# Six pairs of gate projections by seven products, ahead of the linear attention, with the gates parked in DRAM

## The chip, the cores and the metric

The kernel runs on one core of one Trainium2 chip. The metric is the device time of one execution in microseconds, as a median over runs. Engines are named as the profile names them: PE (matmuls), PEld (its weight loads), DVE, ACT, POOL (elementwise work) and SP, whose queue issues the DMAs.

## What is computed

One decoder layer over 1024 tokens of 1024 channels, in float32: a SwiGLU block, a token mixer, a second SwiGLU block, each behind a norm with shift and scale. The change lies in the mixer:

```python
proj = u @ w_in
gq, gk, gv, gr, ga, dq, dk, dv, gates = jnp.split(proj, split_points(IN_SIZES), axis=-1)
ya = gla(gq, gk, gv, ga, gla_alpha_w2, gla_alpha_b)
ya = rmsnorm(ya, gla_head_norm) * jax.nn.silu(gr)...
ya = ya.reshape(B, S, GLA_VW) @ w_branch_a
yb = diff_attention(dq, dk, dv, lq1, lk1, lq2, lk2, lam_init)
yb = rmsnorm(yb, diff_head_norm) * (1.0 - lam_init)
yb = yb.reshape(B, S, DIFF_VW) @ w_branch_b
g_a, g_b = jnp.split(jax.nn.sigmoid(gates), N_BRANCH, axis=-1)
return (g_a * ya + g_b * yb) @ w_out
```

`gates` has 2048 columns: 8 groups of 128 for branch 0 (the linear attention, `ya`) and 8 for branch 1 (the differential attention, `yb`).

## The kernel before

Everything is kept channel-major: a tile has 128 channels as partitions and tokens as columns, in two halves `hf` of 512 tokens. Each float32 operand of a large matmul is split in two numbers, `hi` (rounded) and `lo` (the rest), and a product takes three matmuls (hi by hi, hi by lo, lo by hi). A **unit** is 128 output columns of weights against all tokens: 8 groups `k` of channels, 3 products, 2 halves, 48 matmuls of 128x512 (`project`, L2457; matmuls at L2468). Its weights are loaded by SP into one of three slots of `w_raw` (L766), and POOL makes `w_hi` (L997) and `w_lo` (L1003, two instructions) of a slot once the unit that held it is done (`split_unit`). SP issues the load of unit u once unit u-3 is split.

The two SwiGLU blocks multiply with the seven-product scheme instead (Strassen's, in Winograd's form): a pair of column groups is one tile of seven products of 12 matmuls each (L2507), 84 where two units would take 96. It needs sums of the token blocks once (T1 to T4, made by DVE, ACT and POOL) and, for each tile, four sums of weights, seven roundings (ACT, L1297), seven `lo` (POOL, L1030) and some additions of the results. The first weights of a tile can be loaded only when POOL has read those of the tile before.

The mixer, in order. `norm(1)`: DVE makes the normalized pieces, ACT rounds them to `u_hi`, and DVE (even k, L1809) and POOL (odd k, L1051) make `u_lo`. PE begins on them at once in `first_units` (L2419): the narrow projection `ga` and the two units of `gq`, half 0 and then half 1, k by k, each k behind its `u_lo`. Then 16 small matmuls of the decay (`z`, L2604), the units of `gk` and `gv`, the linear attention, the differential attention with further units as filling, and the branches.

The branches: `branch_product(br, m)` is 24 matmuls of a branch's output against the columns m of its weights; one split of weights serves two m. It alternates with gate units: for each pair of m first the two gate units (L2468), then the two branch products. Gates (0,0) to (0,2) are made earlier. ACT takes the sigmoid of a gate out of PSUM (L1649), DVE multiplies it with the branch product (L2338 for branch 0, L2341 for branch 1) and for branch 1 adds both branches in `z[m]` (L2343). Between the branches ACT rounds the four blocks of `yb` (`high_y`, L1411) once the last product of branch 0 is done, because they take the place of `ya`'s, and DVE makes their `lo` (`low_y`, L2059). Late in branch 1, before m=6, DVE makes `lo` of z[0] to z[5] (`low_z`, L2059), and of z[6], z[7] at the end; the output projection `w_out` follows k by k behind it.

Each engine works through its instructions in the written order. SP writes the residual `h` (4 MB) to DRAM near the start of the mixer (L917) and reads it back among the branches (L931).

Of the kernel before, what the change touches and what calls it, by code (L numbers as in the profile page):

```python
# [13 lines left out]
P = 128  # L14
# [36 lines left out]
U_OUT = U_BRANCH + 24  # L51
# [3 lines left out]
for _br in range(2):  # L55
    for _i in range(0 if _br else 2, 4):
        _order += [("gate", _br, 2 * _i), ("gate", _br, 2 * _i + 1), ("w", _br, _i)]
BRANCH_UNIT = {what: U_BRANCH + n for n, what in enumerate(_order)}
MB = 0
MIX_LOADS = MIX_UNITS // SLOTS  # L60
# [17 lines left out]
def build_program(nc, a, out):  # L78
    ctx = ExitStack()
    with ctx:  # L80
# [86 lines left out]
        with stage() as st_:  # L167
            at(st_, "pad_out", [P, FRONT // 4])
            o_tile = [at(st_, f"o_tile{j}", [P, D])[:] for j in range(8)]
        u2_b, u3_b, g0_b, g1_b = [bufs[:, j, :] for j in range(4)]  # L170
# [18 lines left out]
        un_b = [far[:, j * HALF:(j + 1) * HALF] for j in (14, 15, 16, 17)]  # L189

        def un_place(n, hf, k):

            if n == 1:
                return un_b[piece(n, hf, k) % 4]
            return unf[:, hf + 2 * (k // 4), k % 4, :]
# [24 lines left out]
        low = far[0:2 * GLA_RANK + 1, 5 * S:6 * S]  # L220
# [40 lines left out]
        sig_b = [far[:, 4 * S + j * HALF:4 * S + (j + 1) * HALF] for j in range(2)]  # L261
        h_dram = nc.dram_tensor("h_dram", (P, KT * S), F32).ap()
# [20 lines left out]
        h_dve = sem("h_dve")  # L283
        root_ready = sem("root_ready")
        half_in = [sem(f"half_in{j}") for j in range(2)]
# [122 lines left out]
        gains_ready = sem("gains_ready")  # L408
        y_t = sem("y_t")
# [85 lines left out]
        Z_BANK = (4, 5, 0, 1)  # L495
# [225 lines left out]
        def mix_loads(u):  # L721

            return ffn_loads(u % SLOTS) + u // SLOTS + 1
# [20 lines left out]
        def narrow(w, part=0):  # L744

            return w[:, U_GA, :].rearrange("p (k m) -> p k m", k=KT)[:, :, part * GLA_RANK:(part + 1) * GLA_RANK]

        def t_raw_place(what, i):

            return {"T1": unf[:, 0, i], "T3": unf[:, 1, i], "T2": unf[:, 3, i], "T4": t4_raw[:, i]}[what]  # L750

        def t_place(what, i):

            hi, lo = {"T1": T1, "T2": T2, "T3": T3, "T4": T4}[what]
            return hi[:, i, :], lo[:, i, :]
# [3 lines left out]
        def _(sp):  # L759
            def columns(u, w, c):  # L760

                if u < SLOTS:
                    sp.wait_ge(hs_ready, tile_hs(0, LAST) + 7)
                else:
# [93 lines left out]
            def ffn(f):  # L858
# [16 lines left out]
                sp.wait_ge(tlo_dve, len(T_DVE) * (f + 1))  # L875
                sp.wait_ge(tlo_pool, len(T_POOL) * (f + 1))
# [2117 lines left out]
```

## Time and profile before

| | us |
|---|---|
| median of 3 runs | 2192.16 (2186.67 to 2193.24) |
| profiled execution, its own time | 2192.37 |
| its span | 2190.6 |
| PE busy in it | 2145.7 (98%) |
| POOL, DVE, ACT busy | 1308.0, 1297.3, 817.3 |
| granted TensorE clock, mean | 0.992 |

The profiled execution is 0.2 us above the median. Starts are in us from the start of the span. In a timeline row the busy time of a group counts overlapping matmuls: they are started about 0.227 us apart although each lasts 0.39 us. The places used below are: the end of the first SwiGLU block and `norm(1)` at 690 to 741 us, the linear attention from 790 us, the branches at 1209 to 1440 us, the second SwiGLU block from about 1550 us.

### The profile page before, as it was taken

How to read it: one execution, taken by the hardware profiler on the slowest of the kernel's cores; microseconds unless marked ns; L12 is line 12 of the kernel's file. 1: busy time of each engine (PE TensorE's matmuls, PEld its weight loads, DVE VectorE, ACT ScalarE, POOL GpSimd, SP SyncE). 2: the span in 40 equal slices, each digit the busy share in tenths (PEclk: the TensorE clock that was granted, in tenths of full speed). 3: DMA queues.
4: the chain of work that ended last, by engine and by line, in shares of the span. 5: the costliest groups of instructions: out<-in, count | busy, mean ns of one | idle time of the engine just before them, and what ended most of it. 6: DMA issues, size and time to landing. Idle time of an engine off the chain costs nothing.

```text
span 2190.6 us, 28163 instructions
## 1 busy us (share of the span) xinstructions
PE 2145.7 (98%) x10363; PEld 1766.8 (81%) x10363; DVE 1297.3 (59%) x1987; ACT 817.3 (37%) x1521; POOL 1308.0 (60%) x1042
## 2 busy tenths in 40 slices
PE   7999999999999999999999999999999999999998
PEld 6878788887888777778888888888778888888787
DVE  6956667768966328766666111243955444458955
ACT  7422233224445414355555110023533322334444
POOL 6888788878964432322212333335887888769942
PEclk8999999999999999999999999999999999999999
DMA  7155555558333410011111113111153333356333
GB/s 280 54 167 160 174 159 162 186 175 292 92 102 96 145 49 2 1 39 39 30 30 39 39 48 126 51 50 44 42 170 111 116 101 116 101 210 208 97 97 116
DMA packets 224154, 236.28 MB, mean 108 GB/s; under 512 B 9983, under 2 KB 154514, under 8 KB 223762
## 3 DMA queue, kind: packets, MB, share of 16 engines
q1 hardware_dynamic: 223874, 234.23, 33.4%
q8 instruction: 83, 1.36, 0.3%
q14 instruction: 53, 0.43, 0.1%
q10 hardware_dynamic: 144, 0.26, 0.0%
HBM read 185.69 MB, written 48.76 MB: 107 GB/s over the span
## 4 chain that ended last, share of the span: by engine, by line
PE 75%; DVE 8%; POOL 6%; DMA 3%; ACT 3%; issue 3%; SPq 1%; DVEq 0%; POOLq 0%; ACTq 0%
PE ps L2507 25%; PE ps L2564 16%; PE ps L2405 14%; PE ps L2468 12%; POOL w_lo L1030 3%; DMA ada_half<-in_w_ada 2%; PE ps L2765 1%; DVE x_op L1956 1%; DMA w_raw<-in_ffn_w_in 1%; PE ps L2652 1%; DVE h L2183 1%; PE ps L2730 1%; SPq L798 1%; PE ps L2454 1%; PE ps L2938 1%
## 5 line engine op out<-in xcount | busy, mean ns | idle before, releaser
L2507 PE MATMUL ps<-t,w_hi 128*128 128x512 f32 x1280 | 398.1, 392 | 3.6 <-POOL w_lo L1030 2.6
L1030 POOL TENSOR_TENSOR w_lo<-w_raw,w_hi 128x512 fp32r<-128x512 f32 x240 | 349.5, 1467 | 63.8 <-ACT w_hi L1297 63.2
L2564 PE MATMUL ps<-x_op,w_hi 128*128 128x512 f32 x1232 | 381.0, 390 | 3.3 <-DVE x_op L1956 2.6
L997 POOL TENSOR_SCALAR w_hi<-w_raw 128x1024 fp32r<-128x1024 f32 x55 | 59.1, 1074 | 446.8 <-PE ps L2405 270.0
L1297 ACT ACTIVATE w_hi<-w_raw 128x512 fp32r<-128x512 f32 x240 | 143.9, 625 | 395.0 <-POOL w_raw L1116 174.3
L2507 PEld LDWEIGHTS ps<-t,w_hi 128*128 128x128 f32 x1280 | 240.5, 189 | 56.5 <-POOL w_lo L1030 3.3
L2564 PEld LDWEIGHTS ps<-x_op,w_hi 128*128 128x128 f32 x1232 | 230.7, 188 | 54.7 <-POOL w_lo L1030 4.5
L1030 POOL TENSOR_TENSOR w_lo<-q,w_hi 128x512 fp32r<-128x512 f32 x132 | 197.2, 1502 | 107.4 <-ACT w_hi L1297 107.4
L2507 PE MATMUL ps<-t,w_lo 128*128 128x512 f32 x640 | 250.1, 391 | 0.0
L2564 PE MATMUL ps<-x_op,w_lo 128*128 128x512 f32 x616 | 239.7, 389 | 0.0
L1956 DVE TENSOR_TENSOR x_op<-x_raw,x_op 128x512 fp32r<-128x512 f32 x154 | 177.1, 1162 | 80.1 <-ACT x_op L1307 79.1
L2507 PE MATMUL ps<-b_low,w_hi 128*128 128x512 f32 x640 | 197.3, 390 | 1.9 <-POOL w_lo L1030 1.4
L1769 DVE SCALAR_TENSOR_TENSOR ada_acc<-ada_half,c_act,ada_acc 128x512 f32<-128x512 f32 x98 | 120.9, 1244 | 102.0 <-DMA ada_half<-in_w_ada 102.0
L1307 ACT ACTIVATE x_op<-x_raw 128x512 fp32r<-128x512 f32 x154 | 97.3, 632 | 223.6 <-PE ps L2564 201.3
L1003 POOL TENSOR_TENSOR w_lo<-w_raw,w_hi 128x512 fp32r<-128x512 f32 x124 | 169.9, 1391 | 9.3 <-ACT w_hi L1340 4.2
L2405 PE MATMUL ps<-u_hi,w_hi 128*128 128x512 f32 x384 | 155.9, 406 | 2.0 <-ACT far L1507 1.0
L2405 PE MATMUL ps<-u_lo,w_hi 128*128 128x512 f32 x384 | 150.2, 391 | 0.0
L2405 PE MATMUL ps<-u_hi,w_lo 128*128 128x512 f32 x384 | 149.9, 390 | 0.0
L2507 PEld LDWEIGHTS ps<-b_low,w_hi 128*128 128x128 f32 x640 | 119.8, 188 | 27.9 <-issue 2.3
L2507 PEld LDWEIGHTS ps<-t,w_lo 128*128 128x128 f32 x640 | 120.8, 189 | 25.6
L2564 PEld LDWEIGHTS ps<-x_op,w_lo 128*128 128x128 f32 x616 | 115.6, 188 | 24.0
L2507 PE MATMUL ps<-b_low,w_lo 128*128 128x512 f32 x320 | 124.5, 389 | 0.0
(314 smaller groups left out, 4257.5 us busy)
## 6 DMA issues: line engine op xcount, KB each, us to landing
w_raw<-in_ffn_w_in SPq DMA_DIRECT2D x88, 512.0 KB, 4.3
hid_dram<-hid_raw SPq DMA_DIRECT2D x154, 256.0 KB, 5.1
x_raw<-hid_dram SPq DMA_DIRECT2D x154, 256.0 KB, 2.7
ada_half<-in_w_ada SPq DMA_DIRECT2D x112, 256.0 KB, 2.8
w_raw<-in_w_in SPq DMA_DIRECT2D x41, 512.0 KB, 3.9
q<-in_ffn_w_out SPq DMA_DIRECT2D x6, 1536.0 KB, 9.0
ada_full<-in_w_ada SPq DMA_DIRECT2D x16, 512.0 KB, 12.8
q<-in_ffn_w_out SPq DMA_DIRECT2D x2, 2816.0 KB, 14.2
```

The source lines that it names most:

```text
L798: sp.dma_start(hid_dram[what, t // 2], hid_raw[:, what, :]).then_inc(hid_out, 16)
L997: nc.gpsimd.tensor_scalar(w_hi[:, slot, :], w_raw[:, slot, :], 1.0, 0.0, ALU.mult, ALU.add).then_inc(w_high, 1)
L1003: low_ = nc.gpsimd.tensor_tensor(w_lo[:, slot, half(c)], w_raw[:, slot, half(c)], w_hi[:, slot, half(c)].bitcast(F32), ALU.subtract)
L1030: nc.gpsimd.tensor_tensor(lo, src, hi.bitcast(F32), ALU.subtract).then_inc(hs_ready, 1)
L1297: nc.scalar.activation(hs_place(n)[0], src, ACT.Copy).then_inc(wa_high, 1)
L1307: nc.scalar.activation(x_op[:, n % 3, 0, :], x_raw[:, n % 4, :], ACT.Copy).then_inc(x_high, 1)
L1769: nc.vector.scalar_tensor_tensor(acc, ada_half[:, c, :], c_act[:, k:k + 1], acc, ALU.mult, ALU.add).then_inc(half_used, 1)
L1956: nc.vector.tensor_tensor(x_op[:, n % 3, 1, :], x_raw[:, n % 4, :], x_op[:, n % 3, 0, :].bitcast(F32), ALU.subtract).then_inc(x_ready, 1)
L2405: mm = nc.tensor.matmul(out_, w[i], x[j], start=(start and q == 0), stop=(stop and q == 2))
L2468: mm = nc.tensor.matmul(ps[bank + hf][:], w[:, slot, c], u[:, hf, k, :], start=(k == 0 and u is u_hi and w is w_hi), stop=(k == KT - 1 and ...
L2507: mm = nc.tensor.matmul(ps[bank][:], w[i], x[:, k, :], start=(first and k == 0 and q == 0), stop=(k == 3 and q == 2), skip_group_check=True)
L2564: mm = nc.tensor.matmul(ps[down_bank(p) + m][:], w[:, tile(m)], x_op[:, n % 3, x, :], start=(p in (0, 1, 3) and k == 0 and q == 0), stop=( ...
```

## The change

Of the 13 gate units among the branches, gate (0,3) stays and the other twelve go. They are made right after the units of `gk`, as six tiles of seven products each (`gate_tile`), with the same kind of token sums as the SwiGLU blocks have (`token_sums(1)`, into new buffers `unm`, `m_t1h` and so on). The order of the mixer on PE is now: `first_units`, the two `gk` units, six gate tiles, `z`, the four `gv` units, the linear attention. ACT writes the sigmoids, SP writes each to `gate_dram` (512 KB a gate, twelve) and reads them back during the branches into `u_lo` and `keep`, which are free then; the read of `h` moves behind these reads. The narrow weights of `ga` get a tile of their own (`ga_w`), so that slot 0 is free for the first `gk` unit, and its split moves up in POOL's order.

```diff
                 elif n == 1:
                     pool.wait_ge(w_high, U_GA + 1)
-                    nc.gpsimd.tensor_tensor(narrow(w_hi, 1), narrow(w_raw), narrow(w_hi).bitcast(F32),
+                    nc.gpsimd.tensor_tensor(narrow(ga_w, 1), narrow(w_raw), narrow(ga_w).bitcast(F32),
...
                     nc.gpsimd.memset(low, 1.0).then_inc(low_init, 1)
+                    split_unit(U_GK)
...
+            def gate_tile(t):
+
+                g0, g1, u0, u1 = gate_halves(t)
...
+                nc.gpsimd.tensor_tensor(gs_raw, g0, g1, ALU.add).then_inc(gate_sum, 1)
+                nc.gpsimd.tensor_tensor(g0, u0, g0, ALU.subtract).then_inc(gate_sum, 1)
+                gate_low_hs(n, u0)
+                pool.wait_ge(gate_sum, gate_sum_at(t, 2))
+                nc.gpsimd.tensor_tensor(u0, gs_raw, u0, ALU.subtract).then_inc(gate_sum, 1)
...
+                gate_low_hs(n + 1, u0)
+                gate_low_hs(n + 2, g0)
+                gate_low_hs(n + 3, gs_raw)
...
+                gate_low_hs(n + 4, u1)
+                nc.gpsimd.tensor_tensor(u1, u1, u0, ALU.subtract).then_inc(gate_sum, 1)
+                gate_low_hs(n + 5, g1)
+                pool.wait_ge(gate_sum, gate_sum_at(t, 4))
+                gate_low_hs(n + 6, u1)
...
+        def gate_raw_free(engine, j):
+
+            if j < SLOTS:
+                engine.wait_ge(w_split, U_GV - SLOTS + j + 1)
+            else:
+                c = j - SLOTS
+                engine.wait_ge(gate_low, GATE_LOW + 7 * (c // 2) + 6 + c % 2)
...
+            def gate_product(n, block, bank, first):
+
+                pe.wait_ge(gate_low, GATE_LOW + n + 1)
+                w_h, w_l = gate_place(n)
+                hi, lo = block
+                for k in range(4):
+                    for q, (w, x) in enumerate(((w_h, hi), (w_h, lo), (w_l, hi))):
+                        mm = nc.tensor.matmul(bank[:], w[:, tile(k)], x[:, k, :], start=(first and k == 0 and q == 0),
...
+                nc.vector.tensor_tensor(gu2_b, gu2_b, b[1][:], ALU.add).then_inc(gate_step, 1)
...
+                pe.wait_ge(sig_ready, 2 * EARLY - 2)
+                u = BRANCH_UNIT["gate", 0, EARLY]
+                project(MB + u, u % SLOTS, 2 + 4 * (EARLY % 2)).then_inc(unit_done, 1)
                 for br in range(2):
-                    for m in range(KT):
-                        if (br, m) >= (0, EARLY):
-                            n = 2 * KT * br + 2 * m
-                            pe.wait_ge(sig_ready, n - 2)
-                            u = BRANCH_UNIT["gate", br, m]
-                            project(MB + u, u % SLOTS, 2 + 4 * (m % 2)).then_inc(unit_done, 1)
-                        if m % 2 == 1 and (br, m) > (0, 1):
-                            branch_product(br, m - 1)
-                            branch_product(br, m)
+                    for m in range(0 if br else 2, KT):
+                        branch_product(br, m)
```

The first two pieces are POOL's (`norm(1)` and the weights of a gate tile), then SP's wait before a load of gate weights, PE's product, the first of DVE's five additions of a tile, and PE's branches. `high_y` and `low_y` of the second branch and the places of `low_z` in DVE's order are as they were.

POOL in `norm(1)`, from the middle of half 0 to the first split after half 1. Before:

```order
L997 TENSOR_SCALAR w_hi<-w_raw 128x1024
L1003 TENSOR_TENSOR w_lo<-w_raw,w_hi 128x512 x2
L1051 TENSOR_TENSOR u_lo<-far,u_hi 128x512
L1073 MEMSET far 33x1024
L1051 TENSOR_TENSOR u_lo<-far,u_hi 128x512 x4
```

and with the change:

```order
L1146 TENSOR_SCALAR w_hi<-w_raw 128x1024
L1152 TENSOR_TENSOR w_lo<-w_raw,w_hi 128x512 x2
L1200 TENSOR_TENSOR u_lo<-unm,u_hi 128x512
L1222 MEMSET far 33x1024
L1146 TENSOR_SCALAR w_hi<-w_raw 128x1024
L1152 TENSOR_TENSOR w_lo<-w_raw,w_hi 128x512 x2
L1200 TENSOR_TENSOR u_lo<-unm,u_hi 128x512 x4
```

The split of the first `gk` unit (L1146, L1152) now stands ahead of the four `u_lo` of half 1.

ACT in the branches: sigmoids of gates (L1649, later L1904), `high_y` of the second branch (rar<-h) and `high_z` (u_hi<-far). Before:

```order
L1642 ACT_TABLE_LOAD
L1642 ACTIVATE far<-far 128x512 x6
L1649 ACTIVATE far<-ps 128x512 x10
L1411 ACTIVATE rar<-h 128x1024 x4
L1649 ACTIVATE far<-ps 128x512 x14
L1411 ACTIVATE u_hi<-far 128x512 x12
```

and with the change:

```order
L1897 ACTIVATE far<-far 128x512 x6
L1904 ACTIVATE far<-ps 128x512 x2
L1607 ACTIVATE rar<-h 128x1024 x4
L1607 ACTIVATE u_hi<-far 128x512 x16
```

Only one gate's two sigmoids are left there.

PE at the same place, end of branch 0 (ps0, ps1). Before, a gate unit (ps2, ps3) stands between the branches:

```order
L2405 MATMUL ps0<-rar,w_hi 128x512 x2
L2405 MATMUL ps0<-rar,w_lo 128x512
L2405 MATMUL ps1<-rar,w_hi 128x512 x2
L2405 MATMUL ps1<-rar,w_lo 128x512
L2468 MATMUL ps2<-u_hi,w_hi 128x512
L2468 MATMUL ps3<-u_hi,w_hi 128x512
```

and with the change the next product, of m even (ps4, ps5), follows at once at every such place:

```order
L2694 MATMUL ps0<-rar,w_hi 128x512 x2
L2694 MATMUL ps0<-rar,w_lo 128x512
L2694 MATMUL ps1<-rar,w_hi 128x512 x2
L2694 MATMUL ps1<-rar,w_lo 128x512
L2694 MATMUL ps4<-rar,w_hi 128x512 x2
L2694 MATMUL ps4<-rar,w_lo 128x512
```

## Rows read from the trace of the kernel before

**Rows 1.** The page: the span, and busy time, share and count of PE.
```profile
span 2190.6 us, 28163 instructions
PE 2145.7 (98%) x10363; PEld 1766.8 (81%) x10363; DVE 1297.3 (59%) x1987; ACT 817.3 (37%) x1521; POOL 1308.0 (60%) x1042
```

**Rows 2.** Waits of PE, whole span, one of the mixer: total, times, longest.
```profile
PE ps L2411 <- DVE far L1866: 1.0, 1, 1.0
```

**Rows 3.** Timeline of PE: start and length in us; first matmuls after stage changes.
```profile
1407.02 0.62 PE L2468 MATMUL ps<-u_hi,w_hi 128*128 128x512 f32 x2
...
1428.78 0.62 PE L2405 MATMUL ps<-rar,w_hi 128*128 128x512 f32 x2
```

**Rows 4.** Timeline of POOL and DVE in tiles of the second SwiGLU block.
```profile
1706.05 1.30 POOL L1112 TENSOR_TENSOR s_raw<-w_raw 128x512 f32<-128x512 f32 x1 [2.38 <-DMA w_raw<-in_ffn_w_in]
...
1714.46 1.31 POOL L1030 TENSOR_TENSOR w_lo<-s_raw,w_hi 128x512 fp32r<-128x512 f32 x1
1715.71 1.76 POOL L1030 TENSOR_TENSOR w_lo<-w_raw,w_hi 128x512 fp32r<-128x512 f32 x1
...
1724.58 1.29 POOL L1112 TENSOR_TENSOR s_raw<-w_raw 128x512 f32<-128x512 f32 x1 [2.91 <-DMA w_raw<-in_ffn_w_in]
...
1715.25 1.07 DVE L2002 TENSOR_TENSOR hid_raw<-bufs 128x512 f32<-128x512 f32 x1
```

**Rows 5.** Waits of PE from 1560 to 1680 us, start of that block.
```profile
PE ps L2507 <- POOL w_lo L1030: 3.7, 5, 1.4
```

**Rows 6.** SP's DMAs at 713 us: issue, time to landing; the page's median for that kind.
```profile
L917 SPq DMA_DIRECT2D h_dram<-h x1: 351/351/351, 713.4 to 713.4; - x1
...
L766 SPq DMA_DIRECT2D w_raw<-in_w_in x1: 437/437/437, 713.8 to 713.8; - x1
...
DMA to landing us min/median/max: 15.0/15.0/15.0
...
w_raw<-in_w_in SPq DMA_DIRECT2D x41, 512.0 KB, 3.9
```

**Rows 7.** Timeline of POOL and PE around half 1 of the norm.
```profile
718.21 0.94 POOL L1073 MEMSET far<- 33x1024 f32 x1
724.41 1.30 POOL L1051 TENSOR_TENSOR u_lo<-far,u_hi 128x512 fp32r<-128x512 f32 x1 [5.26 <-ACT far L1266]
...
740.01 1.05 POOL L997 TENSOR_SCALAR w_hi<-w_raw 128x1024 fp32r<-128x1024 f32 x1 [7.08 <-PE ps L2426]
...
743.61 1.04 POOL L997 TENSOR_SCALAR w_hi<-w_raw 128x1024 fp32r<-128x1024 f32 x1
...
728.25 0.39 PE L2426 MATMUL ps<-u_hi,w_hi 128*32 128x512 f32 x1
```

**Rows 8.** PE after a stall, and windows: length, busy by engine (instructions), PEclk, DMA.
```profile
45.89 1.19 PE L2405 MATMUL ps<-b_low,w_hi 128*128 128x512 f32 x2 [4.49 <-DVE b_low L1841]
...
48.00:52.00 4.00, 4.00 (x11) 3.08 (x11) 4.00 (x4) 3.94 (x7) 4.00 (x3) 0.56 0.28 85
...
716.00:720.00 4.00, 2.80 (x10) 1.22 (x9) 2.72 (x3) 0.88 (x2) 2.17 (x2) 1.00 0.91 393
```

**Rows 9.** Timelines of PE, ACT and DVE between the branches.
```profile
1309.10 0.62 PE L2468 MATMUL ps<-u_hi,w_hi 128*128 128x512 f32 x2
...
1309.30 3.91 ACT L1411 ACTIVATE rar<-h 128x1024 fp32r<-128x1024 f32 x4 [3.52 <-PE ps L2405]
...
1310.51 6.83 DVE L2059 TENSOR_TENSOR rar<-h,rar 128x1024 fp32r<-128x1024 f32 x4
```

**Rows 10.** Timeline of DVE and PE late in branch 1.
```profile
1374.58 0.69 DVE L2341 TENSOR_TENSOR far<-far,ps 128x512 f32<-128x512 f32 x1 [2.70 <-PE ps L2405]
...
1429.64 9.88 DVE L2059 TENSOR_TENSOR u_lo<-far,u_hi 128x512 fp32r<-128x512 f32 x12 [19.01 <-ACT u_hi L1411]
...
1446.22 2.49 DVE L2059 TENSOR_TENSOR u_lo<-far,u_hi 128x512 fp32r<-128x512 f32 x4
...
1439.66 0.62 PE L2468 MATMUL ps<-u_hi,w_hi 128*128 128x512 f32 x2
```

More of the change, by code:

```diff
@@ L54 @@
 _order = [("gate", 0, m) for m in range(EARLY)] + [("w", 0, 0), ("gate", 0, 3), ("w", 0, 1)]
-for _br in range(2):
-    for _i in range(0 if _br else 2, 4):
-        _order += [("gate", _br, 2 * _i), ("gate", _br, 2 * _i + 1), ("w", _br, _i)]
+_order += [("w", _br, _i) for _br in range(2) for _i in range(0 if _br else 2, 4)]
 BRANCH_UNIT = {what: U_BRANCH + n for n, what in enumerate(_order)}
 MB = 0
-MIX_LOADS = MIX_UNITS // SLOTS
+GATES = [(0, m) for m in range(EARLY + 1, KT)] + [(1, m) for m in range(KT)]
+GATE_TILES = len(GATES) // 2
+GATE_STEPS = 5
+MIX_LOADS = (MIX_UNITS + len(GATES)) // SLOTS
 STEPS = 7
@@ L1225, in unit_high @@
                 if u == U_GA:
[L1226 removed]
+                    nc.scalar.activation(narrow(ga_w), narrow(w_raw), ACT.Copy).then_inc(w_high, 1)
                 else:
@@ L1273, in t_high @@
                     t_lowered(act, q, "T1", i)
-                nc.scalar.activation(t_place(what, i)[0], t_raw_place(what, i), ACT.Copy).then_inc(thi_ready, 1)
+                if q == 1 and what == "T4":
+                    t_lowered(act, q, "T3", i)
+                nc.scalar.activation(t_place(q, what, i)[0], t_raw_place(q, what, i), ACT.Copy).then_inc(thi_ready, 1)
             def high_hs(n):
@@ new lines, in gates, with t_highs @@
+            def gates():
+                def t_highs(what):
+                    for i in range(4):
+                        t_high(1, what, i)
+                t_highs("T2")
+                gate_hs(0)
+                t_highs("T1")
+                t_highs("T3")
+                gate_hs(1)
+                t_highs("T4")
+                for n in range(2, HS_SLOTS):
+                    gate_hs(n)
+                for t in range(GATE_TILES):
+                    gate_tile(t)
+                nc.scalar.preload_act_table_set("natural_log_exp_and_others")
+                act.wait_ge(gate_used, GATE_USED + 7 * GATE_TILES)
@@ L1419, in mixer @@
                     copy(gq[0][:, half(hf)], ps[2 + hf][:], gqk_act, GLA_DK ** -0.5)
+                act.wait_ge(unit_done, MB + U_GQ + 2)
+                for hf in range(2):
+                    copy(gq[1][:, half(hf)], ps[6 + hf][:], gqk_act, GLA_DK ** -0.5)
+                gates()
+                act.wait_ge(z_done, 4)
                 for b in range(4):
-                    act.wait_ge(z_done, b + 1)
                     nc.scalar.activation(la_b[b], ps[Z_BANK[b]][:], ACT.Abs).then_inc(abs_ready, 1)
@@ L1431, in mixer @@
                     copy(rar[:, b * HALF:(b + 1) * HALF], la_b[b], lahi_ready, 1.0 / GLA_TAU)
-                act.wait_ge(unit_done, MB + U_GQ + 2)
-                for hf in range(2):
-                    copy(gq[1][:, half(hf)], ps[6 + hf][:], gqk_act, GLA_DK ** -0.5)
                 act.wait_ge(lalo_ready, 4)
+                act.wait_ge(gate_out, GATE_OUT + 16 * len(GATES))
                 for hd in range(GLA_H + 1):
@@ L1798, in un_of @@
                     dve.wait_ge(rstd_ready, 2 * n + hf + 1)
-                if n == 1 and j >= piece(1, 0, 4):
-                    dve.wait_ge(ulo_pool if k % 2 else ulo_dve, j // 2 - 1)
                 nc.vector.scalar_tensor_tensor(un_place(n, hf, k), root_place(n, hf), scale_c[:, n, k:k + 1],
```

416 lines of the change are left out of this document (324 added, 92 removed).

## Prediction

> **What bounds the kernel now.** I read the page first: PE is busy for 2145.7 of 2190.6 us [rows 1]. Then the waits of PE: the longest ones stand at the start of the program, and in the mixer the longest is the 1.0 us of one on DVE [rows 2]. So PE sets the time, and matmuls that go are worth their full spacing, as long as nothing new makes PE wait. The rest is the search for such waits, at the four places where the new order puts PE behind another engine: half 1 of the second norm, the gate tiles, the seam between the branches, and the end of branch 1.
>
> **What goes.** Two gate units, 96 matmuls, fill PE from 1407.02 to 1428.78 us, 21.76 us, or 0.227 us a matmul [rows 3]. Twelve units are 576 matmuls and 130.6 us. Six tiles of 84 are 504 matmuls at the same shape and spacing, 114.2 us. That is 16.3 us less on PE, and PE is the path. All else of the move (`z`, the `gk` and `gv` units, gate (0,3), all branch products) has the same matmuls as before, some in another place. The dip of the clock behind `z` moves with `z`, and costs what it did.
>
> **Half 1 of the norm.** In POOL's new order the split of the first `gk` unit stands ahead of the four `u_lo` of half 1. It needs the raw weights. Their load is issued at 713.8 us, 0.4 us behind the 4 MB write of `h`, and lands 15.0 us later, at 728.8, where such a load has a median of 3.9 [rows 6]. Before, nobody needed it until 740.01, when POOL split it. POOL is through with its memset at 719.2 and then made the first `u_lo` of half 1 at 724.41 [rows 7]. Now it stands still until 728.8, splits for 3.6 us (740.01 to the next split at 743.61 [rows 7]) until 732.4, and the `u_lo` follows 1.3 us later, at 733.7. PE wants that piece (k=1) at 728.25 [rows 7]. With 0.1 us for the hand-over it stands for 5.5 us. The other three `u_lo` follow every 1.3 us and PE wants one per two k, which is 16 matmuls or 3.6 us, so it is one wait, not four. Bounds: 5.3 if the split meets no other traffic, 6.5 if DVE slows POOL (one `lo` of 1.76 instead of 1.3 us [rows 4]).
>
> The wait also touches the clock. After the wait of 4.49 us that ended at 45.89 the first two matmuls took 1.19 us instead of 0.62, and from 48 to 52 us the granted clock was 0.56 and 11 matmuls ran where 17.6 fit [rows 8]. So the clock stood at its lower level (1.2 GHz) for 2.1 us up to 48 and some 3.5 us behind it, and half of these 5.6 us was lost. In 716 to 720, with waits of 1.0 us and less, the clock stayed at 1.00 [rows 2, 8]. A wait of 5.5 us is nearer to the first row: I take 2.5 us, bounds 0 and 3.2 (a little over the row, for a longer wait).
>
> **The start of the gate tiles.** PE reaches them two units (21.8 us) after `first_units`. In these POOL must split the second `gk` unit (3.6), make its four token sums (5.2 to 7.0) and two `lo` of them (about 3.5, with ACT in between), and for the first product two sums of weights and one `lo` (3.9 to 5.2). Together 16.2 to 19.3 us, from the end of `first_units` on, since the split waits for the slot that the `gq` unit held. That is 2.5 to 5.6 us ahead of PE. The second and third product need another `lo` about each 2.7 us, which is PE's rate, after a further sum and a `lo` of T3. The nearest row of such a start is the second SwiGLU block, where PE waited 3.7 us in five waits for this very instruction of POOL [rows 5]. There DVE works beside POOL all the time, on sums with two operands in SBUF; here it makes the first sums while POOL still waits for `first_units`. I take 0.5 us; bounds 0 and 3.7.
>
> **The gate tiles themselves.** Their rhythm is that of the SwiGLU tiles: load the weights of which the slot has just come free, then two sums, `lo`, sum, five `lo`, sum, a `lo`, and then the next load. In the trace this loop runs from 1706.05 to 1724.58, 18.5 us [rows 4], against 19.0 us that PE needs for 84 matmuls, so POOL waits for its load (2.4 and 2.9 us) and PE for nobody. Here the loop has the same parts, with less of DVE: five additions a tile, each with one operand in PSUM. ACT has seven roundings, a copy and four sigmoids, 12 instructions of about 0.6 us in 19. The writes of the gates are 1 MB a tile, and SP waits for the last sigmoid, about 2 us after the tile's end, before it issues the next loads; these wait for POOL's `lo` anyway, some 6 us after the tile's start. Cost taken: 0.
>
> **The small-matmul stage behind the tiles.** The chain from `z` through ACT and DVE (absolute value, exponential, logarithm, minimum, rounding) was covered by three units and is covered by two `gv` units now, 21.8 us for a chain of about 12 us. The splits of the `gv` units are due 4 us after the last tile at the earliest, and their slots come free from 11 us before its end. Cost 0.
>
> **The seam of the branches.** Before, PE went from the last product of branch 0 into a gate unit at 1309.10. Behind it ACT rounded the four blocks of `yb`, one a microsecond, and DVE made two products and then the four `lo` from 1310.51 to 1317.34 [rows 9], all under 21.8 us of gates. Now the first product of branch 1 comes at once, and its k-th quarter (six matmuls, 1.36 us) needs the k-th `lo`. The last quarter cannot begin before 1317.4 and ends at 1318.8 at the earliest, where 24 matmuls from 1309.10 would end at 1314.5. POOL splits weights at the same moment as before, so the four `lo` are no faster, and the second and third, slowed by it, end so late that the last quarter has to wait for its turn too: I take 4.5 us, bounds 2.5 (DVE and POOL apart) and 5. It is one wait of 2.7 and two of about 0.9. For the clock this lies between the wait that cost nothing and the one that cost 2.8 [rows 8]; I take 1.2 us, bounds 0 and 2.5.
>
> **The end of branch 1.** DVE needs 3.4 us for a pair of halves (from 1374.58), against 5.4 us of PE for a product, so it keeps up. But before m=6 stand twelve `lo` of z. They took 9.9 us beside POOL's split, and ended at 1439.5, 0.2 us before PE began the output projection at 1439.66; then m=6 and m=7 took 6.7 us, and the `lo` of z[6] were due at 1447.4, 0.4 us before PE wanted them [rows 10]. Now they cannot start before m=5 is done, 3.6 us after its product. With most of the split past by then they take 8.5 us and end about 1.2 us after PE has begun the projection instead of 0.2 before. The lead of 0.4 turns into a wait of 0.8 us; bounds 0 and 2.
>
> **DMAs.** SP reads the first four gates back as soon as gate (0,3) is done, 16 us before DVE wants the first. Four reads of 512 KB are half of the 4 MB write that cleared in 15 us. The read of `h` is issued behind `low_y`, about where it was, and the next weights behind it are wanted 40 us later. Cost 0.
>
> **The sum.** -16.3 + 5.5 + 2.5 + 0.5 + 4.5 + 1.2 + 0.8 = -1.3 us, on the profiled execution's own 2192.4, which is 0.2 above the median of 2192.2. So 2191.0 us. The change takes 72 matmuls off PE and gives nearly all of them back as waits.
>
> **Rivals.**
> *The first split is hidden.* The Trainium skill ("DMA: Bandwidth & Descriptors", Queues, rings and completion order) says that completion is not first in, first out for one issuing engine. By that rule the load could land before the write of `h`. If the load of 512 KB takes its median of 3.9 us, it lands at 717.7, POOL splits from 719.2 to 722.8, before it could start the `u_lo` anyway, and the 8.0 us of this place go: 2183.0. Against it speaks the landing of 15.0 us for that very load in this trace [rows 6], which the change leaves in its place; the same page also says that each engine takes descriptors in ring order. Chance 0.12.
> *POOL can't feed the gate tiles.* The loop has ten POOL instructions and some 5 us of load and hand-overs. At 1.30 us each it takes 18 us; at 1.40 it passes PE's 19.0. At the 1.76 of the stretched row [rows 4] it would be 22.6, and if half of them are stretched 20.3: 1.3 us a tile, 6 to 8 in all, and with the full 3.7 of the start [rows 5] 10 to 12: 2201, slower than before. For it speaks the 1.76, which ran beside a DVE sum of two operands in SBUF (1715.25); against it the 1.31 right before, and that the gates have no such sum. The Trainium skill ("GPSIMD Engine Reference", Specifications) names two SBUF inputs of a DVE instruction as what contends with POOL; the gates' additions have one. By that rule this rival falls. Chance 0.12.
> *The clock stays up.* Neither wait costs more than itself: 2187.3. This is within the forecast's own range, and 0.15 of its chance.
>
> **How the numbers follow.** The forecast, with or without its clock terms, has 0.76, and its own range is 2185 to 2197. The range that should hold 8 times in 10 takes in the first rival's 2183 and most of the second: 2183 to 2199. A measurement here can tell about 0.3% (6.6 us) from no change. Faster by more than that (below 2185.6) is the first rival and the lower edge of the forecast: 0.20. Slower (above 2198.7) is the second and the upper edge: 0.12. The same: 0.68.
>
> **What the profile after would show.** A wait of PE of 5 to 6 us in `first_units` on a `u_lo` of POOL, and POOL idle for 9 us ahead of it on a load of `w_raw`. The tiles 19.0 us apart, with POOL waiting for loads. A wait on `low_y` near 2.7 us, two small ones, and less than 1 us on the last `lo` of z. PE's count 72 lower. Wrong would be: no wait at the norm, or tiles further apart than 19.5 us, or a wait on a gate that comes back from DRAM.

## The result: 3.7 us slower, where 1.3 us faster was forecast

| | before | changed |
|---|---|---|
| median of 19 runs each, us | 2189.56 (2185.91 to 2195.36) | 2193.96 (2187.60 to 2197.17) |
| profiled execution, its span | 2190.6 | 2194.6 |

The ratio is 1.0017, with a 95% interval of 1.0009 to 1.0024: 3.7 us slower, 2.0 to 5.3. That is inside the range given and less than the 0.3% that was called "the same", but the interval lies clear of no change, on the side that was not forecast.

The page of the changed kernel, beside [rows 1] (span; busy time, share and count of PE), and four rows of its waits of PE over the whole span (total, times, longest), beside [rows 2]:

```profile
span 2194.6 us, 28299 instructions
PE 2137.9 (97%) x10291; PEld 1755.8 (80%) x10291; DVE 1345.1 (61%) x2042; ACT 854.6 (39%) x1587; POOL 1367.6 (62%) x1080
```

```profile
PE ps L2715 <- POOL u_lo L1200: 6.4, 1, 6.4
...
PE ps L2694 <- DVE rar L2311: 2.9, 2, 2.6
...
PE ps L2807 <- POOL w_lo L1308: 0.3, 1, 0.3
PE ps L2757 <- DVE u_lo L2311: 0.2, 1, 0.2
```

PE has its 72 matmuls less and is 7.8 us less busy, and yet the span is 4.0 us longer. The four waits are the four that the prediction named: the norm, the seam, the start of the gate tiles, the end of branch 1. What they don't explain lies where it did not look. The table splits both profiles at the same instructions of PE (length of each stage in us; twelve gate units, 130.6, are taken out of the stages of before in which they stood):

| stage | before | changed | forecast | found |
|---|---|---|---|---|
| up to `first_units` | 709.3 | 706.9 | 0 | -2.4 |
| `first_units` | 31.8 | 40.4 | +8.0 | +8.5 |
| twelve gates as units or tiles | 130.56 | 114.63 | -15.8 | -15.9 |
| from `z` to the linear attention (less two `gk` units) | 53.6 | 55.2 | 0 | +1.6 |
| linear attention | 117.3 | 120.5 | 0 | +3.2 |
| branches without those gates | 98.4 | 103.3 | +5.7 | +4.8 |
| output projection, to the first fast tile of the second SwiGLU block | 132.3 | 132.8 | +0.8 | +0.5 |
| from there to the end | 618.6 | 621.9 | 0 | +3.3 |

The row of the gates goes from the first to the last start of their 504 matmuls; up to the start of `z` it is 114.95, so the like-for-like gain is 15.6. The rows found add up to 3.6, and with that 0.3 to 3.9 of the 4.0. The first row is chance: over all sixteen profiles of this case it lies between 704.6 and 710.6 without the change and between 705.4 and 709.3 with it. The last row is not, and it is most of the miss.

### The profile page after: what moved, and what is told of

It is laid out like the page before. It is cut to its first block, busy times and chain, and to the rows that moved or that the text cites. A ratio compares the mean times of both kernels' runs of the same rounds, so it can differ in the third digit from the quotient of the medians.

```text
span 2194.6 us, 28299 instructions
## 1 busy us (share of the span) xinstructions
PE 2137.9 (97%) x10291; PEld 1755.8 (80%) x10291; DVE 1345.1 (61%) x2042; ACT 854.6 (39%) x1587; POOL 1367.6 (62%) x1080
## 4 chain that ended last, share of the span: by engine, by line
PE 67%; DVE 11%; POOL 8%; DMA 5%; issue 4%; ACT 3%; SPq 2%; ACTq 0%; DVEq 0%; POOLq 0%
PE ps L2796 25%; PE ps L2898 14%; PE ps L2694 13%; PE ps L2757 5%; PE ps L2807 4%; POOL w_lo L1179 3%; DVE x_op L2208 2%; DMA ada_half<-in_w_ada 2%; PE ps L3108 1%; DMA w_raw<-in_ffn_w_in 1%; PE ps L2995 1%; DVE h L2467 1%; PE ps L3073 1%; DMA x_raw<-hid_dram 1%; DVE h L2264 1%
## 5 line engine op out<-in xcount | busy, mean ns | idle before, releaser
L1179 POOL TENSOR_TENSOR w_lo<-w_raw,w_hi 128x512 fp32r<-128x512 f32 x240 | 354.7, 1489 | 53.0 <-ACT w_hi L1493 51.9
L1146 POOL TENSOR_SCALAR w_hi<-w_raw 128x1024 fp32r<-128x1024 f32 x43 | 47.0, 1093 | 377.5 <-PE ps L2694 280.8
L2208 DVE TENSOR_TENSOR x_op<-x_raw,x_op 128x512 fp32r<-128x512 f32 x154 | 184.6, 1213 | 76.5 <-ACT x_op L1503 75.4
L2023 DVE SCALAR_TENSOR_TENSOR ada_acc<-ada_half,c_act,ada_acc 128x512 f32<-128x512 f32 x98 | 115.3, 1188 | 106.8 <-DMA ada_half<-in_w_ada 106.8
L1152 POOL TENSOR_TENSOR w_lo<-w_raw,w_hi 128x512 fp32r<-128x512 f32 x100 | 139.1, 1412 | 8.3 <-ACT w_hi L1536 4.2
L2796 PEld LDWEIGHTS ps<-t,w_lo 128*128 128x128 f32 x640 | 120.5, 188 | 25.5
```

Of the source, the lines that this page charges most:

```text
L1146: nc.gpsimd.tensor_scalar(w_hi[:, slot, :], w_raw[:, slot, :], 1.0, 0.0, ALU.mult, ALU.add).then_inc(w_high, 1)
L1152: low_ = nc.gpsimd.tensor_tensor(w_lo[:, slot, half(c)], w_raw[:, slot, half(c)], w_hi[:, slot, half(c)].bitcast(F32), ALU.subtract)
L1179: nc.gpsimd.tensor_tensor(lo, src, hi.bitcast(F32), ALU.subtract).then_inc(hs_ready, 1)
L2023: nc.vector.scalar_tensor_tensor(acc, ada_half[:, c, :], c_act[:, k:k + 1], acc, ALU.mult, ALU.add).then_inc(half_used, 1)
L2208: nc.vector.tensor_tensor(x_op[:, n % 3, 1, :], x_raw[:, n % 4, :], x_op[:, n % 3, 0, :].bitcast(F32), ALU.subtract).then_inc(x_ready, 1)
L2796: mm = nc.tensor.matmul(ps[bank][:], w[i], x[:, k, :], start=(first and k == 0 and q == 0), stop=(k == 3 and q == 2), skip_group_check=True)
```

## The norm: a load behind a write

SP, POOL and PE in the changed kernel, in timelines (start, length, then the idle time before it and its releaser), where before showed [rows 6] and [rows 7]:

```profile
710.97 0.35 SPq L1059 DMA_DIRECT2D h_dram<-h  x1
711.37 9.36 SPq L869 DMA_DIRECT2D w_raw<-in_w_in  x2
```

```profile
726.72 1.05 POOL L1146 TENSOR_SCALAR w_hi<-w_raw 128x1024 fp32r<-128x1024 f32 x1 [10.02 <-DMA w_raw<-in_w_in]
727.85 2.80 POOL L1152 TENSOR_TENSOR w_lo<-w_raw,w_hi 128x512 fp32r<-128x512 f32 x2
730.61 6.78 POOL L1200 TENSOR_TENSOR u_lo<-unm,u_hi 128x512 fp32r<-128x512 f32 x4
```

```profile
732.37 0.64 PE L2715 MATMUL ps<-u_hi,ga_w 128*32 128x512 f32 x1 [6.40 <-POOL u_lo L1200]
```

This is the chain as forecast: POOL idle for 10.0 us on the load, the split, then the `u_lo` that PE waited 6.4 us for. That matmul takes 0.64 us, where one takes 0.39 elsewhere: the clock is at its lower level (1.2 GHz), and 2.1 of the 8.5 us are that.

**e1_split_late** does the split behind the norm.

```diff
                     nc.gpsimd.memset(low, 1.0).then_inc(low_init, 1)
-                    split_unit(U_GK)
...
             norm(1)
+            split_unit(U_GK)
             split_unit(U_GK + 1)
```

> The change, with one move on POOL: the split of the first gk unit stands behind the four u_lo of half 1 again. In the profile of the change PE waits 6.4 us there and then works at half clock for a while; first_units takes 40.6 us where it took 32.1. Theory A (the split's place alone makes this): first_units back to 32 to 33 us, 8.0 to 8.5 us less than the change, so 3.5 to 5.5 us under the kernel before (ratio 0.9975 to 0.9985). Rival B (the u_lo of half 1 are late for another reason, the larger new buffers or the load): the wait stays over 3 us and the ratio stays at 1.001 to 1.002. Rival C (the time is given back by the gate tiles, whose token sums and weights then have less cover): first_units short, but new waits of 3 us or more at the first gate products.

Measured: ratio to before 0.9978 (0.9969 to 0.9987), 8.5 us below the changed kernel. `first_units` took 31.8 us, and the gate tiles took 1.1 us longer (115.8 instead of 114.6), with three waits on `w_lo` in place of one, since POOL now makes the split in the time that it needs for their sums.

**e3_early_alone** is the other way round: the kernel before, with only `ga_w` and the early split.

```diff
+        sm("keep", [P, 4, HALF])
+        ga_w = sm("ga_w", [P, KT, 2 * GLA_RANK], F32R)
...
                     nc.gpsimd.memset(low, 1.0).then_inc(low_init, 1)
+                    split_unit(U_GK)
...
-            straight(3, U_HEAD + SLOTS - 3)
+            straight(4, U_HEAD + SLOTS - 4)
```

> The kernel before with nothing of the gates moved, only the split of the first gk unit put ahead of the four u_lo of half 1 on POOL (and the narrow weights of ga in their own tile, as this needs). Theory A: one wait of 5.5 to 6.4 us in first_units and a clock at half for some us behind it, 7.5 to 9 us longer than the kernel before, ratio 1.0034 to 1.0042. Rival C (part of the wait is covered by what follows): under 5 us. If the clock's part is chance by run, the ratio lies nearer to 1.0027 (the wait alone).

Measured: 1.0039 (1.0026 to 1.0052), 8.5 us above before, with a wait of PE of 5.4 us in a `first_units` of 38.9; that is 7.1 us more than before, which the interval (5.7 to 11.4 us) allows. So the early split alone carries the term, and no gate is needed for it.

**g3_load_first** leaves the early split and takes away what makes the load late: the write of `h` goes behind the load.

```diff
+                if u == SLOTS:
                     sp.dma_start(h_dram, h[:].rearrange("p k s -> p (k s)")).then_inc(spill, 16)
```

> The changed kernel with SP's 4 MB write of h behind the load of the first gk weights instead of ahead of it. Theory A (the split waited for the load, and the load for the write): the load lands within 5 us, the split is done before the u_lo of half 1 could start, first_units falls from 40.4 to 40.8 us to 31.9 to 32.5, the gate tiles stay at 114.6, and the time is 8.5 us (7 to 9.5) below the changed kernel, 2184 to 2186. Theory B (a load of these weights is slow there whatever stands ahead, since the write starts at once behind it): it lands 10 us or more after its issue, and first_units keeps 38 us or more; time as the changed kernel, 2192 to 2195.

Measured: 0.9970 (0.9957 to 0.9983), 10.3 us below the changed kernel, of which `first_units` gives 8.5; the interval allows the 8.5 alone. SP's and POOL's timelines:

```profile
713.38 0.39 SPq L869 DMA_DIRECT2D w_raw<-in_w_in  x1
713.81 0.58 SPq L1060 DMA_DIRECT2D h_dram<-h  x1
```

```profile
718.17 0.94 POOL L1223 MEMSET far<- 33x1024 f32 x1
719.10 1.04 POOL L1147 TENSOR_SCALAR w_hi<-w_raw 128x1024 fp32r<-128x1024 f32 x1
720.22 2.55 POOL L1153 TENSOR_TENSOR w_lo<-w_raw,w_hi 128x512 fp32r<-128x512 f32 x2
724.38 1.30 POOL L1201 TENSOR_TENSOR u_lo<-unm,u_hi 128x512 fp32r<-128x512 f32 x1 [1.60 <-ACT unm L1461]
```

The load is issued 0.4 us ahead of the write instead of 0.4 behind it and lands in 4.3 us instead of 15.3. POOL splits right behind its memset and is done before the piece for the next `u_lo` exists: 31.9 us in `first_units`, 114.8 in the gate tiles. The early split was no mistake in itself; what cost was the place of its load in SP's queue. The Trainium skill ("DMA: Bandwidth & Descriptors", Queues, rings and completion order) says both that a DMA engine takes descriptors in ring order and that completion is not first in, first out. This pair agrees with the first; the second, on which a rival rested, bought nothing here.

## The seam

DVE and PE in the changed kernel at the end of branch 0, where before showed [rows 9]:

```profile
1391.64 1.28 DVE L2627 TENSOR_TENSOR far<-u_lo,ps 128x512 f32<-128x512 f32 x2 [4.16 <-PE ps L2694]
1392.85 6.79 DVE L2311 TENSOR_TENSOR rar<-h,rar 128x1024 fp32r<-128x1024 f32 x4
```

```profile
1394.21 0.70 PE L2694 MATMUL ps<-rar,w_hi 128*128 128x512 f32 x2 [2.60 <-DVE rar L2311]
...
1396.35 1.22 PE L2694 MATMUL ps<-rar,w_hi 128*128 128x512 f32 x2 [0.29 <-DVE rar L2311]
...
1399.67 0.61 PE L2694 MATMUL ps<-rar,w_hi 128*128 128x512 f32 x2
```

One wait of 2.6 us on the first `lo` and 0.3 on the second. The two waits of 0.9 did not come in this profile. In their place PE was slow: at 1396.35 two matmuls take 1.22 us instead of 0.61, which is the lower clock again, so that the third and fourth `lo` were ready when it got to them. The wait and the clock were added in the forecast (4.5 + 1.2 = 5.7); they overlap, and 4.8 is found. The same kernel profiled again (f2_after_again below) shows the other half of this: there the clock stays up, and the two small waits do come.

```profile
1393.04 0.74 PE L2694 MATMUL ps<-rar,w_hi 128*128 128x512 f32 x2 [0.52 <-DVE rar L2311]
...
1395.27 0.73 PE L2694 MATMUL ps<-rar,w_hi 128*128 128x512 f32 x2 [0.55 <-DVE rar L2311]
```

Its branches took 103.0 us, against 103.3: either the waits or the lower clock, for about the same price, and not both.

**e2_seam** lets ACT and DVE make two of the four `hi` and `lo` while branch 0 still runs, and PE takes those two first.

```diff
-                        act.wait_ge(unit_done, MB + BRANCH_UNIT["w", 0, 3] + 1)
                         act.wait_ge(yb_ready, 2 * DIFF_H)
-                        for j in range(4):
+                        for j in (2, 3):
+                            high_y(1, j)
+                        act.wait_ge(unit_done, MB + BRANCH_UNIT["w", 0, 3] + 1)
+                        for j in (0, 1):
                             high_y(1, j)
...
+                        if (br, m) == (0, 6):
+                            for j in (2, 3):
+                                low_y(1, j)
...
-                    for k in range(4):
+                    for at_, k in enumerate((2, 3, 0, 1) if br else range(4)):
```

> The change, with the seam of the branches reordered: blocks 2 and 3 of yb, which lie elsewhere than those of ya, are rounded and their lo made before the last product of branch 0, and the first product of branch 1 takes its blocks in the order 2, 3, 0, 1. Theory A: the 2.9 us of waits there shrink to under 1 us, and where the clock fell after them it stays up: from the start of gate (0,3) to the output projection 88 to 89 us instead of 91.9 (87.0 is what the matmuls take), ratio to the kernel before 1.000 to 1.0008. Rival: the waits come from the branch's other work (the gates that come back, the split of weights), and remain within 1 us of what they were, ratio 1.0015 and up.

Measured: 1.0001 (0.9990 to 1.0012), 3.5 us below the changed kernel; the branches took 99.4 us instead of 103.3. Of the 4.8 us at most 1.0 is left, with a wait of 0.6 on that `lo`.

**e4_all_three** is e1, e2 and two of the `low_z` moved ahead of the product before.

```diff
+                        if (br, m) == (1, 5):
+                            low_z((0, 1))
                         if (br, m) == (1, 6):
-                            low_z(range(6))
+                            low_z(range(2, 6))
```

> The change with both moves and a third: of the lo of z that stand ahead of m=6 in branch 1, two are made ahead of m=5. If the losses add as in the profile of the change: 8.3 us at the norm, 3.5 us at the seam, 0.5 us at the end, 12 us less than the change, so 8 us less than the kernel before, ratio 0.996 (0.9955 to 0.997). If they hide one another, or a new wait takes their place, 0.9975 and up.

Measured: 0.9962 (0.9949 to 0.9974), 12.0 us below the changed kernel. The stage of the output projection fell from 132.8 to 132.3, the value of before. So the losses of norm, seam and end of branch 1 add up. Yet the last stage still took 622.5 us.

## The second SwiGLU block: where PE's instructions come in

Nothing in the last stage was edited, and still it took 620.7 to 622.5 us in the four profiles with the change so far and 618.6 in the two without. Two pieces of it differ: the `down` part (PE's loss there against the profile of before, from 0.8 to 2.4 us), and the time behind the last matmul (7.6 to 7.8 instead of 6.2). Four kernels, each profiled once and not timed further, asked what belongs to the kernel and what to the execution.

> The kernel before, unchanged, to see how its stages repeat. Open is where 1.6 to 3.2 us behind the gate tiles and 3.3 us in the second SwiGLU block come from. Profile of before: the linear attention 117.3 us with the clock at 1.2 GHz for 3.4 us at its start, the second SwiGLU block from its first tile 618.6 us, of which 6.2 lie behind the last matmul. Theory P (they belong to the kernel): all of these repeat within 0.3 us. Theory R (they differ by run): the lower clock is 6.8 us here, the linear attention 119 to 120.5, or the down stage of the second block moves by 1 us or more.

> The changed kernel, unchanged. Its profile has 120.5 us in the linear attention (clock lower for 6.8 us at its start and 3.4 at its end), 55.2 from z to there, and 621.9 us in the second SwiGLU block, of which 7.6 behind the last matmul. Theory P: repeats within 0.3 us. Theory R: the linear attention between 117.3 and 120.5, the down stage different by 1 us or more.

Measured: the kernel before again 619.1 us with 6.2 behind the last matmul, the changed one again 621.9 with 7.6. The last stage belongs to the kernel. The linear attention took 117.3 and 118.6 us: that of the changed kernel, 120.5 in its first profile, does not repeat.

**f3_tiny_dmas**: the kernel before with 24 small DMAs more on SP.

```diff
+                if 3 <= u < 15:
+                    for j in (2 * u - 6, 2 * u - 5):
+                        sp.dma_start(tiny_dram[j], a["w_in"][0][j:j + 1, 0:P]).then_inc(tiny, 16)
```

> The kernel before with 24 DMAs more on SP's queue, 512 bytes each from DRAM to DRAM, two behind each load of unit 3 to 14; SP waits for them before the second SwiGLU block. All kernels with the change have 24 DMAs more on SP than before (656 for 632), and 7.6 to 7.8 us behind the last matmul where kernels without have 6.2; there one issue of an output takes 1.1 to 1.6 us of SP where the one 24 earlier in before took 0.33. Theory N (it is the number of DMAs that SP has issued): 7.6 us behind the last matmul here too. Theory T (what the gates themselves leave, their memory or their code): 6.2. Neither expects a change in the mixer; time 2190 to 2192.

Measured: 6.2 us behind the last matmul, 619.0 in the stage. It is not the number of DMAs.

**f4_gate_dram_last** moves one declaration behind two others.

```diff
-        gate_dram = nc.dram_tensor("gate_dram", (len(GATES), P, S), F32).ap()
         h_dram = nc.dram_tensor("h_dram", (P, KT * S), F32).ap()
         hid_dram = nc.dram_tensor("hid_dram", (7, PAIRS, P, HALF), F32).ap()
+        gate_dram = nc.dram_tensor("gate_dram", (len(GATES), P, S), F32).ap()
```

> The changed kernel with gate_dram declared behind h_dram and hid_dram instead of ahead of them, so that these two lie in DRAM where they lay before. In the down stage of the second block DVE waited 7.9 us for three loads of hid_dram in the profile after (2.8 us in one before), and PE lost 1.9 us to its x_op. Theory M (the place in DRAM makes the loads slower): PE's loss in the down stage goes, 0.3 us or less against before. Theory R (it differs by run): 0 to 2.4 us, as in the other kernels with the change. The time behind the last matmul stays 7.6 for both.

Measured: 621.4 and 7.6, with 1.4 us of PE lost in `down`, where 0.3 or less was expected of a place in DRAM. It is not that either.

What was left is PE's program itself. The page lists the DMAs that bring instructions; here are the rows of q8 (packets, MB, share) in before and, with 130 PE instructions more, in g1_before_pad, which is told below:

```profile
q8 instruction: 83, 1.36, 0.3%
```

```profile
q8 instruction: 84, 1.38, 0.3%
```

83 packets of 16 KB go with the 21,367 records of PE, 257 a packet, and 130 more made it 84. The change takes 144 records from PE (72 matmuls and their weight loads) and adds 18 waits. So half a packet is missing, and every packet behind these instructions falls at another place of the work. The view of DMAs shows it, in 3 us around the last matmul (2185 to 2188 in the changed kernel, then 2182 to 2185 in before):

```profile
q1 hardware_dynamic: 319, 1.18, 100.1%
q8 instruction: 1, 0.02, 1.8%
```

```profile
q1 hardware_dynamic: 331, 1.22, 102.5%
```

In the changed kernel a packet of instructions comes 1.1 us before the last matmul starts, in the middle of the output's DMAs; in before it came 16.2 us before it, when the DMA engines were free. The outputs that SP and ACT wrote there, with their time to landing, first before, then changed:

```profile
out_h<-o_tile ACTq DMA_DIRECT2D x1, 256.0 KB, 4.3
out_h<-o_tile SPq DMA_DIRECT2D x1, 256.0 KB, 4.7
```

```profile
out_h<-o_tile ACTq DMA_DIRECT2D x1, 256.0 KB, 5.4
out_h<-o_tile SPq DMA_DIRECT2D x1, 256.0 KB, 6.0
```

Two kernels test it, by moving the packets and nothing else. PE gets waits for a semaphore that has long come, three ahead of each of some 120 matmuls in the first SwiGLU block. By the counts on the pages this adds 130 instructions to the kernel before and 125 to the changed one.

```diff
                     for q, (i, x) in enumerate(((0, hi), (0, lo), (1, hi))):
+                        if 0 <= 12 * (n - 50) + 3 * k + q < 124:
+                            for _ in range(3):
+                                pe.wait_ge(hs_ready, n + 1)
```

> The kernel before with 130 PE instructions more: waits for a semaphore that has long come, ahead of 124 matmuls of ten products in the first SwiGLU block. PE's instructions come by DMA in packets of 16 KB, 83 in a run, and the 144 instructions that the change takes from PE's program move them against the work: the last one starts 1.1 to 1.3 us before the last matmul in four profiles with the change, 16.2 to 16.9 before it in those without. 130 more move them as far the other way round, since 256 instructions make 16 KB. Theory I (these fetches delay the DMAs of the last stages): the last fetch within 2 us of the last matmul, 7.6 us behind the last matmul instead of 6.2, and PE's loss in the down stage of the second block up from 0 to 0.5 (before) to 1.4 to 2.4. Theory T (it is something else of the change): 6.2 and 0 to 0.5 as in the four profiles without the change.

> The changed kernel with 125 such PE instructions more at the same place, which move the fetches back to where they were before. Theory I: 6.2 us behind the last matmul, 0 to 0.5 lost in the down stage, the second SwiGLU block 618.6 to 619.1 us instead of 620.7 to 622.5. Theory T: stays at 7.6 and 621 to 622. What the waits themselves cost in the first block shows in both runs and is no part of it.

Measured, one profile each, in g1_before_pad: last packet 1.1 us before the last matmul, 7.7 us behind it, the stage 620.5. In g2_after_pad: last packet 16.8 us before it, 6.2 behind it, the stage 618.9. Both landings of the last outputs, g1 and then g2:

```profile
out_h<-o_tile ACTq DMA_DIRECT2D x1, 256.0 KB, 5.4
out_h<-o_tile SPq DMA_DIRECT2D x1, 256.0 KB, 5.9
```

```profile
out_h<-o_tile ACTq DMA_DIRECT2D x1, 256.0 KB, 4.3
out_h<-o_tile SPq DMA_DIRECT2D x1, 256.0 KB, 4.7
```

And the wait of PE on DVE's `x_op` in `down`, from 1960 to 2190 us, in before, changed, g1 and g2:

```profile
PE ps L2564 <- DVE x_op L1956: 1.5, 2, 1.1
```

```profile
PE ps L2898 <- DVE x_op L2208: 2.3, 5, 0.9
```

```profile
PE ps L2567 <- DVE x_op L1956: 2.3, 3, 1.1
```

```profile
PE ps L2901 <- DVE x_op L2208: 1.5, 3, 0.7
```

The kernel before takes on the changed kernel's end and the changed kernel that of before, by padding alone. For the tail this is shown to 0.1 us. For `down` it is shown for the changed kernel (a loss of 1.9 us fell to 0.4); in g1 the wait on `x_op` rose to that of the changed kernel, but the loss at the last matmul was 0.4 (1.1 us lost in `down`, 0.7 gained ahead of it), within what before has by itself, where 1.4 to 2.4 was expected. There the place of the packets is not all. That it also counts how late the work itself is against them is a guess that no run tests.

> The changed kernel with 125 PE instructions more in the first SwiGLU block, as g2_after_pad, timed. Theory I (the place of the fetches costs the changed kernel 2 to 3 us at its end): ratio to before 0.9995 to 1.0008, about 0.001 below the changed kernel's 1.0017. Theory R (the profiles showed run to run differences): 1.0017 again, or above for the added waits.

Measured, over 11 runs: 0.9995 (0.9987 to 1.0004), where the changed kernel has 1.0017 (1.0009 to 1.0024). The intervals don't meet. 125 instructions that do nothing made the changed kernel about 4.8 us faster, and the stage took 619.1, which is 3.0 of them. The other 1.8 lie at the norm: `first_units` took 38.8 and 38.9 us in the two padded kernels that still load behind the write (g2, h1), and 40.4 to 41.0 in the four without padding. DMAs there (for the loads the median time to landing), first in the changed kernel from 711 to 727 us, then in h1 from 713 to 728, with PE's wait:

```profile
q8 instruction: 1, 0.02, 0.3%
w_raw<-in_w_in SPq DMA_DIRECT2D x3, 512.0 KB, 15.3
```

```profile
w_raw<-in_w_in SPq DMA_DIRECT2D x3, 512.0 KB, 13.6
PE ps L2715 <- POOL u_lo L1200: 4.9, 1, 4.9
```

Without padding a packet of PE's instructions falls some 12 us behind the issue of the 4 MB write, and the load behind the write lands after 15.0 to 15.3 us, in all ten such kernels, before among them. With padding no packet falls there, and it lands after 13.6, in g2, h1 and also in g1, the kernel before with padding. So a packet amid the write goes with 1.4 to 1.7 us more for what stands behind it, and padding takes them away in either kernel; only the changed one waits for that load.

## The clock behind z and in the linear attention

PE in stretches of time (length, busy time, granted clock, DMA share, GB/s): the start of the linear attention in before, changed and g3_load_first.

```profile
817.00:827.00 10.00, 8.43 (x52) 0.83 0.20 54
```

```profile
939.00:952.00 13.00, 11.28 (x57) 0.74 0.15 40
```

```profile
931.00:944.00 13.00, 11.45 (x94) 1.00 0.15 42
```

The stage has the same instructions with the same waits (0.8, 0.2, 0.2 and 1.0 us at its start) in all three, and took 117.3, 120.5 and 116.0 us; the difference is the time at 1.2 GHz. In all sixteen profiles: 117.2 to 118.5 us without the change (five profiles, mean 117.5), and 116.0 to 120.5 with it (eleven, mean 119.1). From `z` to there it is 52.0 to 55.2 for both kinds, means 53.3 and 53.6. So of the 4.8 us that this pair of profiles shows, about 1.9 stand in the means, and the rest is one execution against another. The clock fell at the same place of the program, behind the small matmuls and waits at the stage's start, or not at all. What decides between these, and why the changed order gets the longer stretch more often, was not settled; that the two sparse stages now lie 55 us apart instead of 75 is the only difference seen.

## All causes together

**h2_load_seam** is g3, e2 and the two `low_z` of e4; **h3_load_seam_pad** adds the PE instructions of g2.

> The changed kernel with the load of the first gk weights ahead of the write of h (first_units 31.9 instead of 40.4, gate tiles 114.7), the seam of e2 (99.4 instead of 103.0 to 103.3) and two lo of z earlier (132.3 instead of 132.8). If they add up: 8.5 + 3.8 + 0.5 = 12.8 us below the changed kernel, ratio 0.9955 to 0.9965. If the load is what counts alone and the seam moves a wait elsewhere: 0.997 as g3_load_first.

> h2_load_seam with the 125 PE instructions more in the first SwiGLU block. Theory I: the last PE fetch 16 to 17 us before the last matmul, 6.2 us behind it, the second SwiGLU block 618.6 to 619.1 us, and 2 to 3 us below h2_load_seam: ratio 0.9942 to 0.9955. Theory R: as h2_load_seam.

Measured: h2 2182.07 us, 0.9958 (0.9943 to 0.9974); h3 2177.00 us, 0.9940 (0.9924 to 0.9957), with 2190.36 us for before beside them. The stages of h3: `first_units` 31.9, gate tiles 114.6, branches 99.4, output projection 132.3, the end 618.8 with 6.2 us behind the last matmul (h2: 623.4 and 7.8). Its page:

```profile
span 2175.5 us, 28423 instructions
PE 2129.1 (98%) x10291; PEld 1751.8 (81%) x10291; DVE 1345.1 (62%) x2042; ACT 855.5 (39%) x1587; POOL 1360.8 (63%) x1080
```

h3 is 13.1 us below the kernel before (9.4 to 16.6) and 16.9 below the changed one. The 16.3 us of the 72 matmuls were there all the time. The change gave them back at the norm, the seam, the end of branch 1, in the clock of the sparse stages and in the last block, none of which is a matter of the seven products.

## The prediction, point by point

**PE is the path, 72 matmuls are worth 16.3 us.** Right: twelve gates took 114.6 us (115.0 with the step to `z`) instead of 130.6.

**Half 1 of the norm, 5.5 + 2.5.** Right in mechanism, place and size (6.4 + 2.1). It took the landing after 15.0 us as given; 1.4 of these hang on where a packet of instructions falls. The rival that the load is hidden (2183.0) fell. With the write out of its way g3 took 2183.19, but that the two figures agree is luck: the rival is 9.4 us below its own start of 2192.4, and g3 6.6 below the 2189.64 of before beside it.

**Start of the gate tiles, 0.5.** Right: 0.4 to 0.7 in all, by where the stage is taken to end, one wait of 0.3.

**The tiles' rhythm, 0.** Right. In the changed kernel POOL's loop of a tile runs from 802.15 to 819.69, 17.5 us, its instructions at 1.29 to 1.31:

```profile
802.15 1.29 POOL L1318 TENSOR_TENSOR h<-w_raw 128x512 f32<-128x512 f32 x1 [2.77 <-issue]
...
804.64 1.31 POOL L1308 TENSOR_TENSOR w_lo<-w_raw,w_hi 128x512 fp32r<-128x512 f32 x1
...
819.69 1.29 POOL L1318 TENSOR_TENSOR h<-w_raw 128x512 f32<-128x512 f32 x1 [2.80 <-issue]
```

The rival that POOL can't feed them (2201) fell; in these loops there is none of the 1.76 us of [rows 4]. Around the first tile there are: POOL took 1.74 us at 765.42 and 1.75 at 773.18, and beside them ran DVE's token sums, which have two operands in SBUF (`m_t3l<-unm,m_t3h` at 764.23, `m_t<-keep,m_t` from 769.68 to 773.77). That agrees with the rule of the Trainium skill ("GPSIMD Engine Reference", Specifications) by which a DVE instruction with two SBUF inputs contends with POOL: the gates' additions on DVE have one.

**The seam, 4.5 + 1.2.** The wait on the first `lo` was 2.6, forecast 2.7. The sum was 0.9 us too high: the two small waits and the lower clock are one price and not two.

**End of branch 1, 0.8.** 0.5.

**"The dip of the clock behind z moves with z, and costs what it did."** This is one step that failed, though by less than the pair of profiles says: 1.9 us in the means, for that stage and the linear attention behind it. The prediction took the clock's stretches from one profile as if they were a property of the code. Why the mean rose is open.

**The second SwiGLU block.** This is the step that failed and turned the sign. The prediction said that "the rest is the search for such waits, at the four places where the new order puts PE behind another engine", so a stage whose code is the same was put at nothing. It cost 3.2 us (means without padding: 618.8 over the four profiles without the change, 622.1 over the eight with it). Fewer instructions on PE move the packets that bring them; padding gave 3.0 of the 3.2 back.

Without the last two the terms as found give -16.3 + 8.5 + 0.4 + 4.8 + 0.5 = -2.1, near the -1.3 of the forecast; with 1.9 and 3.2 they give +3.0, against +3.7 (2.0 to 5.3) measured.

## What to carry to other kernels

Before a consumer is moved ahead, look at what its load is queued behind: one line of SP's order was worth 8.5 us of `first_units` here, and the split itself cost nothing. Where an order takes the cover from a conversion, convert half of it under the work before. When many instructions leave the program of the busiest engine, later stages can shift by that alone, here by some 3 us: compare unedited stages of both traces first, and try the kernel with as many instructions that do nothing.

## What the runs showed of the hardware

A packet of 16 KB of PE's instructions that arrives amid full output DMAs goes with a landing of the last output after 5.3 to 6.1 us instead of 4.7, and the program ends 1.4 us later. In the sixteen profiles the two always came together: the eight with the change and without padding and g1 have both, the other seven neither. SP's own issue of one output took 0.6 to 1.8 us there instead of 0.33. Amid a 4 MB write such a packet goes with a landing after 15.0 to 15.3 us instead of 13.6 of the load behind the write (ten profiles against three). Satisfied waits ahead of 120 matmuls cost PE nothing that the time up to `first_units` shows (704.6 to 709.1 us with them, 706.6 to 710.6 without). And a 512 KB load issued 0.4 us behind a 4 MB write landed after 15 us, issued 0.4 us ahead of it after 4.3 to 4.5.
